# Second table of a PEER layer on one core: bfloat16 sums of squares, one 2048-column gate multiply, activation halves in 1024-column steps, the inverse-scale product on ScalarE

## What is computed

```
q1, q2 = halves of (xb @ wq), 8 heads
v1, i1 = top_k(q1 . keys1, 16);  v2, i2 = top_k(q2 . keys2, 16)
vals, ci = top_k(v1[..., :, None] + v2[..., None, :], 16)
e = i1[ci // 16] * 128 + i2[ci % 16]
g = softmax(vals)
a = gelu(einsum('nd,nhkd->nhk', xb, u_tab[e]))
y = einsum('nhk,nhkd->nd', g * a, v_tab[e])
```

## Time and profile before

| | us |
|---|---|
| three executions | 2352.74, 2348.49, 2346.95 |
| median | 2348.49 |
| profiled execution, span from first to last instruction | 2342.4 |
| the block between the first and the last of 28 totals, 27 turns | 577.59 |
| TensorE busy in the span | 2186.2 |
| VectorE busy in the span | 1810.6 |
| ScalarE busy in the span | 1251.8 |

### The profile page before, as it was taken

How to read it: one execution, slowest core, us unless ns; L and a number is a source line. 1 busy time by engine, 2 the same in 40 slices (tenths; PEclk the granted TensorE clock), 3 DMA queues, 4 the chain that set the end, 5 groups by cost and what they waited for, 6 DMA issues and landing times. The chain is left out here.

```text
span 2342.4 us, 33509 instructions
## 1 busy us (share of the span) xinstructions
PE 2186.2 (93%) x11984; PEld 1188.4 (51%) x11984; DVE 1810.6 (77%) x3801; ACT 1251.8 (53%) x1675; POOL 431.1 (18%) x395
## 2 busy tenths in 40 slices
PE   6899998998787999999999999989999999999997
PEld 3566666443555674445555555544444444444443
DVE  2576543655677656789999999954899999999999
ACT  1566562425567835643444346766556555655562
POOL 0011110000010210022323233410222222222220
PEclk9899998999899999999999999999999999999999
DMA  9665562000755944478999998895977887788771
GB/s 391 244 215 189 184 218 82 18 19 9 296 187 189 339 184 163 164 252 270 304 345 305 348 312 333 323 368 189 360 280 296 297 302 291 289 309 298 291 280 72
DMA packets 192073, 574.28 MB, mean 245 GB/s; under 512 B 18464, under 2 KB 52032, under 8 KB 184256
## 3 DMA queue, kind: packets, MB, share of 16 engines
q1 hardware_dynamic: 113872, 329.69, 40.4%
q0 software_dynamic: 47104, 167.80, 19.2%
q10 hardware_dynamic: 30960, 75.07, 8.2%
HBM read 455.48 MB, written 117.00 MB: 244 GB/s over the span
## 5 line engine op out<-in xcount | busy, mean ns | idle before, releaser
L297 PE MATMUL u_ps<-h_hi,lin_hi 128*128 128x512 f16 x1024 | 390.0, 381 | 6.4 <-PEq L74 6.4
L297 PE MATMUL u_ps<-h_lo,lin_hi 128*128 128x512 f16 x1024 | 390.0, 381 | 0.0
L297 PE MATMUL u_ps<-h_hi,lin_lo 128*128 128x512 f16 x1024 | 389.9, 381 | 0.0
L279 DVE SCALAR_TENSOR_TENSOR lin_lo<-lin_raw,lin_wsc,lin_hi 128x1024 f16<-128x1024 f32 x132 | 169.3, 1283 | 162.9 <-ACT lin_hi L273 162.5
L1945 POOL DMA_INDIRECT row<-v_dram,picked x128 | 179.1, 1400 | 578.2 <-DVE acc L2580 449.3
L2010 POOL DMA_INDIRECT row<-u_rows_dram,picked x128 | 176.0, 1375 | 520.7 <-DVE dot_junk L2194 354.4
L273 ACT ACTIVATE lin_hi<-lin_raw,lin_wsc 128x1024 f16<-128x1024 f32 x132 | 151.1, 1146 | 184.1 <-DVE lin_wsc L138 138.8
L2451 PE MATMUL ps_w<-oh_turned,oh_buf 128*128 128x128 f16 x1024 | 224.3, 219 | 4.5 <-ACT region L2123 4.5
L2691 PE MATMUL y_ps<-region 128*128 128x512 f16 x512 | 194.7, 380 | 1.4 <-PEq L1949 1.4
L2693 PE MATMUL y_ps<-region 128*128 128x512 f16 x512 | 194.7, 380 | 0.0
L2692 PE MATMUL y_ps<-region 128*128 128x512 f16 x512 | 194.6, 380 | 0.0
(11 more groups left out here) (406 smaller groups left out, 4417.9 us busy)
## 6 DMA issues: line engine op xcount, KB each, us to landing
lin_raw<-w_all_dram SPq DMA_DIRECT2D x132, 512.0 KB
act_scratch<-activated ACTq DMA_DIRECT2D x128, 256.0 KB
wgt_scratch<-region ACTq DMA_DIRECT2D x64, 512.0 KB
region<-v_dram SPq DMA_DIRECT2D x15, 2048.0 KB
oh_buf<-v_dram SPq DMA_DIRECT2D x15, 2048.0 KB, 7.4
proj<-w_mod_dram SPq DMA_DIRECT2D x16, 1536.0 KB
act_buf<-w_all_dram SPq DMA_DIRECT2D x38, 512.0 KB, 7.4
lin_hi<-split_scratch SPq DMA_DIRECT2D x64, 256.0 KB
```

Source lines behind the costliest of these rows:

```text
L279: nc.vector.scalar_tensor_tensor(out=self.lo[b][:], in0=self.raw[b][:], scalar=self.wsc[:, self.col(b)], in1=self.hi[b][:], op0=ALU.mult, ...
L297: last = nc.tensor.matmul(self.ps[b % 2][:, half, 0:ts.stop - ts.start], w_[:, kc, :], x_[:, kc, ts], start=(j == 0 and kc == 0), stop=(j ...
```

## The change

Four edits, all in the handling of the second table:

- `total` multiplies with a bfloat16 matrix of ones, `ones_h`, and reads the upper half of each float32 sum as a bfloat16 number (`upper`). `ones_h` is filled once by VectorE at the program's start.
- `multiply` is one instruction of 2048 columns where there were four of 512. Its pattern has one level more: slab, block of 64 tokens, token.
- `heads_a` and `split_a` work in 2 x 1024 columns where there were 4 x 512. The waits on `vp_a_split`, `vp_a_head` and `vp_mult` count to match.
- `yinv` is made by a ScalarE instruction of one column behind `heads_a`, and no longer by VectorE behind the scales.

```diff
--- before.py
+++ after.py
@@ -116,6 +116,7 @@
         cols = sb(top, "cols", [P, 40])
         ident = sb(top, "ident", [P, P])
         ones = sb(top, "ones", [P, P])
+        ones_h = sb(top, "ones_h", [P, P], BF16)
         hsum = sb(top, "hsum", [P, 4, KC])
         hscale = sb(top, "hscale", [P, 4])
         hinv = sb(top, "hinv", [P, 4])
@@ -136,6 +137,10 @@
                                          ALU.logical_shift_right, ALU.bitwise_and))
             link(nc.vector.tensor_scalar(inv, tmp, 2.0 ** 50, 2.0 ** -70, ALU.mult, ALU.max))
             return nc.vector.reciprocal(scale, inv)
+
+        def upper(sums):
+
+            return sums.bitcast(BF16).rearrange("p (n two) -> p n two", two=2)[:, :, 1]
 
         def act_scale(dve, link, k, ps, done):
 
@@ -406,7 +411,7 @@
                 sp.wait_ge(s(f"vp_v_split{gp}"), VG * i)
                 sp.dma_start(self.v_raw[gp][:, :, :].rearrange("p c d -> p (c d)"),
                              a["v"][:, bass.ds((2 * i + gp) * VG * D, VG * D)]).then_inc(s(f"vp_ld_v{gp}"), 16)
-                sp.wait_ge(s(f"vp_a_split{gp}"), VG * i)
+                sp.wait_ge(s(f"vp_a_split{gp}"), 2 * i)
                 self.load_a(sp, i, gp)
 
             def load_v(self, sp, i, gp, c_):
@@ -430,7 +435,7 @@
                                      accum_out=self.sum[:, gp, 0:1]).then_inc(s(f"vp_sq{gp}"), 1)
 
             def squares_a(self, act, i, gp, other):
-                act.wait_ge(s(f"vp_mult{gp}"), VG * i + VG)
+                act.wait_ge(s(f"vp_mult{gp}"), i + 1)
                 act.wait_ge(s(f"vp_sq{gp}"), 2 * i + 1)
                 act.wait_ge(s(f"vp_sq{1 - gp}"), other)
                 nc.scalar.activation(self.junk[:, 0:VG * NLAT], self.g_act[gp][:, :, :].rearrange("p c n -> p (c n)"), ACT.Square,
@@ -448,26 +453,27 @@
 
             def heads_a(self, act, i, gp):
                 act.wait_ge(s(f"vp_scaled{gp}"), i + 1)
-                for c_ in range(VG):
-                    nc.scalar.activation(self.a_hi[gp][:, c_, :], self.g_act[gp][:, c_, :], ACT.Copy,
+                for c_ in range(0, VG, 2):
+                    nc.scalar.activation(self.a_hi[gp][:, c_:c_ + 2, :], self.g_act[gp][:, c_:c_ + 2, :], ACT.Copy,
                                          scale=self.scale[:, gp, 1:2]).then_inc(s(f"vp_a_head{gp}"), 1)
+                nc.scalar.activation(self.yinv[:, gp:gp + 1], self.inv[:, gp, 0:1], ACT.Copy, scale=self.inv[:, gp, 1:2]
+                                     ).then_inc(s(f"vp_y_inv{gp}"), 1)
 
             def heads(self, act, i, gp):
                 self.heads_v(act, i, gp)
                 self.heads_a(act, i, gp)
 
-            def multiply(self, dve, i, gp, c_):
-                if c_ == 0:
-                    dve.wait_ge(s(f"vp_ld_w{gp}"), 16 * i + 16)
-                    dve.wait_ge(s(f"vp_ld_a{gp}"), 16 * i + 16)
-                col = self.g_act[gp][:, c_, :].rearrange("p (b n) -> p b n", n=WB)
-                nc.vector.tensor_tensor(col, col, self.w_raw[gp][:, :, c_ * WB:c_ * WB + WB], ALU.mult
+            def multiply(self, dve, i, gp):
+                dve.wait_ge(s(f"vp_ld_w{gp}"), 16 * i + 16)
+                dve.wait_ge(s(f"vp_ld_a{gp}"), 16 * i + 16)
+                every = self.g_act[gp][:, :, :].rearrange("p c (b n) -> p c b n", n=WB)
+                nc.vector.tensor_tensor(every, every, self.w_raw[gp][:, :, :].rearrange("p b (c n) -> p c b n", n=WB), ALU.mult
                                         ).then_inc(s(f"vp_mult{gp}"), 1)
 
             def total(self, pe, i, gp):
                 pe.wait_ge(s(f"vp_sq{gp}"), 2 * i + 2)
                 pe.wait_ge(s(f"vp_scaled{gp}"), i)
-                nc.tensor.matmul(self.total_ps[:, gp, :], ones[:], self.sum[:, gp, :], start=True, stop=True
+                nc.tensor.matmul(self.total_ps[:, gp, :], ones_h[:], upper(self.sum[:, gp, :]), start=True, stop=True
                                  ).then_inc(s(f"vp_total{gp}"), 1)
 
             def scales(self, dve, i, gp):
@@ -475,8 +481,6 @@
                 dve.wait_ge(s(f"vp_total{gp}"), i + 1)
                 two_power(link, self.total_ps[:, gp, :], self.tmp[:, gp, :], self.inv[:, gp, :], self.scale[:, gp, :]
                           ).then_inc(s(f"vp_scaled{gp}"), 1)
-                nc.vector.tensor_tensor(self.yinv[:, gp:gp + 1], self.inv[:, gp, 0:1], self.inv[:, gp, 1:2], ALU.mult
-                                        ).then_inc(s(f"vp_y_inv{gp}"), 1)
                 dve.wait_ge(s(f"vp_scaled{gp}"), i + 1)
 
             def split_v(self, dve, i, gp, c_):
@@ -485,10 +489,11 @@
                                                scalar=self.scale[:, gp, 0:1], in1=self.v_hi[gp][:, c_, :],
                                                op0=ALU.mult, op1=ALU.subtract).then_inc(s(f"vp_v_split{gp}"), 1)
 
-            def split_a(self, dve, i, gp, c_):
-                dve.wait_ge(s(f"vp_a_head{gp}"), VG * i + c_ + 1)
-                nc.vector.scalar_tensor_tensor(out=self.a_lo[gp][:, c_, :], in0=self.g_act[gp][:, c_, :],
-                                               scalar=self.scale[:, gp, 1:2], in1=self.a_hi[gp][:, c_, :],
+            def split_a(self, dve, i, gp, n):
+                dve.wait_ge(s(f"vp_a_head{gp}"), 2 * i + n + 1)
+                cs = slice(2 * n, 2 * n + 2)
+                nc.vector.scalar_tensor_tensor(out=self.a_lo[gp][:, cs, :], in0=self.g_act[gp][:, cs, :],
+                                               scalar=self.scale[:, gp, 1:2], in1=self.a_hi[gp][:, cs, :],
                                                op0=ALU.mult, op1=ALU.subtract).then_inc(s(f"vp_a_split{gp}"), 1)
 
         def rolled(eng, nq, slab, first=0):
@@ -836,6 +841,7 @@
                     def _(dve):
                         link = Chain(dve, s("dve1"))
                         nc.vector.memset(csil, 0.0).then_inc(s("csil0"), 1)
+                        nc.vector.memset(ones_h[:], 1.0).then_inc(s("lin_ones_h"), 1)
                         for i in range(NMW):
                             dve.wait_ge(s(f"wm_used{i % NWM}"), i // NWM + 1)
                             if i >= 2:
@@ -978,6 +984,7 @@
                     @block.tensor
                     def _(pe):
                         pe.wait_ge(s("csil"), 1)
+                        pe.wait_ge(s("lin_ones_h"), 1)
                         pe.wait_ge(s("ld_picks"), 32)
 
                         def gather(i):
@@ -2411,18 +2418,16 @@
                 for m in range(NK - TAIL, NK - 3):
                     lin.dve_slab(dve, Q_U + m // 4, m % 4, min(2, (NK - 1 - m) // 4), False)
                     if m == NK - 5:
-                        for c_ in range(VG):
-                            second.multiply(dve, 0, 0, c_)
+                        second.multiply(dve, 0, 0)
                     else:
                         dot(1)
-                for c_ in range(VG):
-                    second.multiply(dve, 0, 1, c_)
+                second.multiply(dve, 0, 1)
                 second.scales(dve, 0, 0)
                 dot(PICKS)
                 for c_ in range(VG):
                     second.split_v(dve, 0, 0, c_)
-                for c_ in range(VG):
-                    second.split_a(dve, 0, 0, c_)
+                for n in (0, 1):
+                    second.split_a(dve, 0, 0, n)
                 second.scales(dve, 0, 1)
 
             @block.tensor
@@ -2590,8 +2595,7 @@
                 def mixed(i, gp, j, ngp):
 
                     rows = rows_of(2 * i + gp)
-                    for c_ in range(VG):
-                        second.multiply(dve, j, ngp, c_)
+                    second.multiply(dve, j, ngp)
                     add_up(i, gp, 0)
                     add_up(i, gp, 1)
                     add_row(next(rows))
@@ -2604,10 +2608,8 @@
                     second.split_v(dve, j, ngp, 3)
                     add_up(i, gp, 4)
                     second.split_a(dve, j, ngp, 0)
+                    add_up(i, gp, 5)
                     second.split_a(dve, j, ngp, 1)
-                    add_up(i, gp, 5)
-                    second.split_a(dve, j, ngp, 2)
-                    second.split_a(dve, j, ngp, 3)
                     add_row(next(rows))
                     add_up(i, gp, 6)
                     add_row(next(rows))
@@ -2623,8 +2625,8 @@
                         second.split_v(dve, 0, 1, c_)
                     add_up(0, 0, 0)
                     add_up(0, 0, 1)
-                    for c_ in range(VG):
-                        second.split_a(dve, 0, 1, c_)
+                    for n in (0, 1):
+                        second.split_a(dve, 0, 1, n)
                     for r in range(2, R):
                         add_up(0, 0, r)
                         for k in rows if r == R - 1 else (next(rows),) if r % 2 else ():
@@ -2678,7 +2680,7 @@
             def _(pe):
                 def products(i, gp, j=None, ngp=None):
                     pe.wait_ge(s(f"vp_v_split{gp}"), VG * i + VG)
-                    pe.wait_ge(s(f"vp_a_split{gp}"), VG * i + VG)
```

(1 more changed line is left out.)

## The result

| | before | after |
|---|---|---|
| median of 4 runs beside each other, us | 2348.81 | 2332.05 |
| lowest and highest | 2346.95, 2352.74 | 2329.53, 2335.20 |
| profiled execution: time, span | span 2342.4 | 2334.14, 2332.3 |

The changed kernel takes 0.9932 of the time [0.9914, 0.9949], 16.8 us less by the medians. The brackets give the interval that holds the ratio with 95%. A second comparison (6 runs of it, 11 of before) gave 2331.65 against 2346.14, a ratio of 0.9937 [0.9925, 0.9949] or 14.5 us. The forecast was 2335.6, a gain of 12.9.

A forecast was written before the change was run, and what follows sets the result against it. The bound was a cycle through VectorE and ScalarE, passing narrowly to TensorE: 27 x 20.78 = 561.1, plus 3.4 and 1.0, is 565.5 us, 12.1 less. With 0.8 outside, 2348.5 - 12.9 = 2335.6 us, range 2328 to 2344.

The forecast's parts named there:

- the cycle: Second table: scales, first head, splits, rows, multiply, squares, total, back to scales, through VectorE and ScalarE; 21.10 or 21.29 us per turn.
- Multiply 2.31, rests 1.28: VectorE, per turn: one multiply of 2.31 us saves 0.18; two pairs of rests at 1.28 each save 0.26.
- Inverse product worth nothing: VectorE's 0.14 us behind the scales go, but the time saved is waited at the first head: counted as nothing.
- The total on the array: TensorE, from total to next matmul: 0.24 us for float32, 0.06 for bfloat16.
- The total on the cycle: From total to scales, 0.42 us: 0.1 off, only in turns where VectorE waits for the total.
- Five rows: Three of the 27 turns carry a fifth row, putting the cycle 1.1 us over TensorE: 3.4 us.
- Late rows: Rows arriving late in the 27 turns of the second table: they stay, about 1.0 us in all.
- Outside: Beyond the 27 turns: three totals ahead save 0.18 each, the tail's last rests save 0.26: 0.8 us.
- From the span to the median: Whole execution: the median of the runs lies 6.1 us above the profile's span, the same distance after; forecast span 2329.5.
- B: Second table: the cycle stays the bound, a turn is 21.0 us, the whole 2341.5 us; chance 0.17.
- C: TensorE: the bfloat16 total costs the array 0.24 us like the float32 one, the whole 2341.0 us; chance 0.07.
- D: VectorE: the new multiply's pattern runs at half rate, 4.6 us instead of 2.3, the whole 2397 us; chance 0.06.

The follow-up runs named there:

- Total alone: The kernel before with only the bfloat16 total added, all else as before: turns of 20.90 and 21.20 us, one run of 2338.16 us.
- without multiply: The changed kernel with the multiply again in four instructions of 512 columns: turns of 20.75 and 20.85 us, one run of 2336.22 us.
- without rests: The changed kernel with heads and rests of the activations again in 4 x 512 columns: turns of 20.75 and 20.99 us, one run of 2333.29 us.
- waits in another order: The kernel before with ScalarE's wait for the multiply moved last of the three ahead of its squares: turns of 21.18 and 21.19 us, one run of 2352.20 us.
- rows evenly, loads later: The changed kernel with eight rows in the first group, four in every other, and the final norm's weights and residual loaded at the end of SyncE's list: 2329.02 us.
- rows evenly: The changed kernel with eight rows in the first group instead of five and four in every other group: median 2328.36 us.
- again: The changed kernel, unaltered, measured once more on the chip of "rows evenly": median 2331.65 us, 27 turns in 568.08 us.

## Why the prediction was right, point by point

- **The bound was the cycle**: right. "Total alone", "without multiply" and "without rests" each make VectorE's part of it the bound again.
- **Multiply 2.31, rests 1.28**: measured 2.29 and 1.28; 0.18 and 0.25 per turn by the runs. The rule of the Trainium skill ("VectorE: DVE Perf Modes", The DRAIN you can't avoid), that the next instruction waits for an empty pipe, would have given 4 x 0.684 = 2.74 for the four and so 0.45 of saving; the trace shows 2.49 and 0.20. The same section adds that a next instruction that is not held starts earlier, which I left out, and which the trace agrees with.
- **Inverse product worth nothing**: right by its size, wrong by its reason. I had 0.14 us saved and waited again at the first head. Nothing was saved: the product stood in the 0.20 us between the reciprocal and `add_up`, which are there without it too, and the wait at the head is 0.49 either way. Its cover on ScalarE is there as said (7.43 us idle ahead of the squares, 7.71 before).
- **The total on the array** was mis-sized at both ends. I took 0.24 for the old and 0.06 for the new, 0.18 of saving; it is 0.14 and 0.03, 0.11 of saving. So TensorE's turn before was 20.86 and not 20.96, and now is 20.75 and not 20.78. The fault lay in the step that priced a total from rows where it had waited; of the old one I had a price without a wait as well, 0.19, and did not use it. Of the two prices for the new one, the 25 ns of the Trainium skill ("TensorE: Matmul & The Clock Gate", Part 1) was nearer than my nearest row.
- **The total on the cycle**: I took 0.1 us off in one kind of turn. "Total alone" shows 0.20 in one kind (21.10 to 20.90) and 0.09 in the other (21.29 to 21.20): 0.145 on average against my 0.05. The scales came 0.42 us behind the total and now come 0.21. That the gain would reach both kinds I had excluded because VectorE seemed to wait in one only the earlier trace rows. It waited in both, 0.07 and 0.2 us, and those waits are what the new total could take away. It cost the forecast nothing, as TensorE hides all of it.
- **The sum.** 27 turns: 561.1 forecast, 560.1 measured (3 runs at 20.75 throughout). Five rows: 3.4 forecast; the three turns are 21.96, 21.90 and 21.90, which is 3.5. Late rows: 1.0 forecast, 2.5 measured (the turns behind are 21.19, 22.20 and 21.36). Together 565.5 against 566.19, which agrees by luck in part: the turns were 1.0 us shorter and the late rows 1.5 longer than forecast. Outside: 0.8 forecast, 0.8 measured, and this too by luck, since the three turns ahead did not lose 0.18 each: against "waits in another order", which has no slow matmuls there, the first is 0.11 longer, and against before the second is 0.18 and the third 0.45 shorter.
- **From the span to the median.** The gain by place was 12.2 where I had 12.9, and the medians show 16.8 and 14.5. The 6.1 us that I took as the distance between span and median are no such thing: the span and the time of one execution are 1.8 us apart (2332.3, 2334.14), so the profiled run of before, at 2342.4, was a short one. That made the span that I forecast, 2329.5, too low against 2332.3, and left the forecast of the median, 2348.5 - 12.9, as it is. What the medians show beyond 12 us has no place that I could find. Two stretches that the change does not touch vary from kernel to kernel: the last matmul on the first loads starts between 78.5 and 85.2 us, and the way from the end of the gate's matmuls to the first total takes 82.7 to 89.7. Neither goes with the edits. The second goes with one idle time of TensorE in it, for which the profile names nothing that is waited for, and with the granted clock behind that: 82.7 us with 2.3 us idle and a clock of 1.00 over 25 us ("rows evenly, loads later"), 89.7 with 6.6 us and 0.86 ("rows evenly"). Before has 87.9 with 5.3, after 88.5 with 5.6 and, again, 83.8 with 3.3. Whole times scatter with the clock too: of the 22 executions of before in the later comparisons, the longest (2354.01) has a mean of 0.971 and the shortest (2337.97) one of 0.979. It stays open whether the 2 to 5 us are such scatter.
- **Rivals.** B: not the case, although the cycle is close; it did come back in each run that undid one of the two merges. C: no, 0.03 and not 0.24. D: no, 2.29 and not 4.6; the level more in the pattern cost nothing that shows.

## What to carry to other kernels

Price an instruction from rows where it did not wait: the cost of a small matmul in the stream fell from 0.24 to 0.14 us once its operand was on time. Where two engines are within 2% of each other, work out both turns, since merging small instructions pays only until the other one takes over: here 0.45 us of 0.6. Short waits have no bracket on VectorE either; compare the distance of two starts with that of the same pair where it runs back to back. And when the regular turn is settled, the irregular ones are next: spreading the rows, seven in the first group with the later loads, took another 5 to 7 us off the profiles, about half of what the change brought.

## What was not expected of the hardware

- A float32 matmul of two columns among 16-bit ones is two records and 0.14 us to the next start, a bfloat16 one 0.03 us; the result reached VectorE 0.31 us and 0.21 us behind the start.
- A wait at the total of up to 0.24 us carries no bracket ("without rests", 0.46 from start to start where 0.22 is the pace), and on VectorE the 0.07 and 0.2 us of before carry none. A distance between starts shows it, an idle time does not.
- TensorE's clock fell to its lower level behind an idle time of 1.4 us (before) and 2.08 us ("rows evenly"), and not behind 1.8 us in after nor 1.99 in "rows evenly, loads later". "Waits in another order" has the same 1.41 us in the same place as before, and "total alone" and "without multiply" have 1.61; in all three the clock stays at 1.00, so the idle time alone does not decide it. Where it fell it cost 1.6 to 1.7 us, and that looks like a cost of the edit until the granted clock is read.
- An indirect gather of 128 rows of 1024 float32 took 10.6 us from issue to use with the DMA engines busy throughout ("rows evenly"). A ring of four buffers gave the row 7.9 us there.
